# VectorE's small form of the wide expert job: limit raised to 160 tokens, work cut to 160 columns

## The reference, cut to what matters

```
def clamped_swiglu(hid):
    x_glu, x_lin = hid[..., ::2], hid[..., 1::2]
    x_glu = jnp.minimum(x_glu, SWIGLU_LIMIT)
    x_lin = jnp.clip(x_lin, -SWIGLU_LIMIT, SWIGLU_LIMIT)
    return x_glu * jax.nn.sigmoid(SWIGLU_ALPHA * x_glu) * (x_lin + 1.0)
...
        xb = h[toks]
        hid = xb @ w1[e] + b1[e]
        yb = clamped_swiglu(hid) @ w2[e] + b2[e]
        return yb * gts[:, None].astype(yb.dtype)
```

## Time and profile before

| what | value |
|---|---|
| median of 3 runs | 2038.56 us (2037.11 to 2043.55) |
| profiled execution, its own time | 2037.2 us |
| span of its trace | 2035.4 us |
| TensorE busy | 1977.3 us, 97% of the span |
| VectorE busy | 1385.7 us, 68% |
| experts' wide jobs, first to last product | 501.6 to 1307.9 us |
| experts' narrow jobs | 1307.9 to about 2020 us |

### The profile page before, as it was taken

The page is one execution under the profiler, slowest core; times in us unless marked ns, Lnnn a source line. Parts: engine busy times, 40 slices in busy tenths (PEclk is TensorE's granted clock), DMA queues, the critical chain, the costliest instruction groups (busy, mean ns, idle before and its releaser), DMA issues.

```text
span 2035.4 us, 29772 instructions
## 1 busy us (share of the span) xinstructions
PE 1977.3 (97%) x10588; PEld 1442.1 (71%) x10588; DVE 1385.7 (68%) x3952; ACT 385.3 (19%) x792; POOL 237.5 (12%) x313
## 2 busy tenths in 40 slices
PE   8999999997999999999999999999999999999996
PEld 5777777774999999999999999844444444444443
DVE  2666666663467777778877677687767776677765
ACT  1323233222012122222222222301101010001100
POOL 0221222221010011111111111100000000000000
PEclk9999999998999999999999999999999999999998
DMA  9311110004875687777888888999999999999992
GB/s 302 108 42 41 41 40 12 30 32 182 297 222 198 237 269 243 271 240 274 275 270 286 297 298 289 339 319 366 372 355 363 367 371 362 354 370 369 369 357 76
DMA packets 232241, 504.22 MB, mean 248 GB/s; under 512 B 7428, under 2 KB 14640, under 8 KB 230016
## 3 DMA queue, kind: packets, MB, share of 16 engines
q1 hardware_dynamic: 218496, 454.93, 62.6%
q0 software_dynamic: 11392, 40.18, 8.1%
q10 hardware_dynamic: 2304, 8.39, 1.0%
HBM read 475.48 MB, written 28.00 MB: 247 GB/s over the span
## 4 chain that ended last, share of the span: by engine, by line
issue 44%; PE 26%; DMA 2%; DVE 2%; POOL 1%; ACT 0%; POOLq 0%; DVEq 0%; ACTq 0%
PE ps_unit L1651 26%; DMA out_dram<-y_rows,idx_cur 2%; POOL x_got L1258 1%; DMA x_got<-h_rows,idx_next 0%; DVE act_T L1480 0%; DVE sig L1478 0%; DVE glu L1470 0%; ACT sig L1341 0%; PE ps_list L1623 0%; POOL carrier L1254 0%; POOL out_dram L1302 0%; POOL out_dram L1270 0%; POOLq L1194 0%; DVE match L1391 0%; DVE reached L1435 0%
## 5 line engine op out<-in xcount | busy, mean ns | idle before, releaser
L1651 PE MATMUL ps_unit<-xT,w_slot 128*128 128x136 f32 (+6 forms) x3840 | 526.6, 300 | 10.3 <-issue 8.7
L1651 PEld LDWEIGHTS ps_unit<-xT,w_slot 128*128 128x128 f32 x3840 | 521.3, 197 | 11.5 <-issue 11.4
L1675 PE MATMUL ps_unit<-w_slot,xT 128*128 128x512 f32 x1088 | 473.9, 593 | 0.0
L1675 PEld LDWEIGHTS ps_unit<-w_slot,xT 128*128 128x128 f32 x1088 | 205.3, 190 | 251.6 <-issue 251.6
L1183 DVE STREAM_TRANSPOSE xT<-x_got 32x256 f32<-32x256 f32 x668 | 291.0, 436 | 13.4 <-DMA x_got<-h_rows,idx_next 4.6
L1651 PE MATMUL ps_unit<-act_T,w_slot 128*128 128x136 f32 (+6 forms) x1920 | 264.1, 299 | 7.2 <-DVE act_T L1480 7.1
L1651 PEld LDWEIGHTS ps_unit<-act_T,w_slot 128*128 128x128 f32 x1920 | 259.4, 191 | 10.4 <-DVE act_T L1480 6.3
L1687 PE MATMUL ps_unit<-w_slot,act_T 128*128 128x512 f32 x544 | 239.3, 592 | 1.3 <-DVE act_T L1183 1.3
L1496 DVE STREAM_TRANSPOSE y_rows<-yT 32x256 f32<-32x256 f32 x396 | 172.6, 436 | 42.9 <-ACT yT L1348 37.6
L1183 DVE STREAM_TRANSPOSE act_T<-act_rows 32x64 f32<-32x64 f32 x816 | 192.6, 236 | 12.2
L1687 PEld LDWEIGHTS ps_unit<-w_slot,act_T 128*128 128x128 f32 x544 | 102.0, 190 | 123.6 <-issue 121.5
(11 more groups left out here) (262 smaller groups left out, 1604.3 us busy)
## 6 DMA issues: line engine op xcount, KB each, us to landing
w_slot<-in_w_dram SPq DMA_DIRECT2D x192, 2048.0 KB, 11.0
b_row<-in_b_dram SPq DMA_DIRECT2D x17, 1024.0 KB, 13.0
b_row<-in_b_dram SPq DMA_DIRECT2D x17, 512.0 KB, 15.3
w_in_sb<-in_w_in_dram SPq DMA_DIRECT2D x6, 1024.0 KB, 11.9
x_in<-in_x_dram SPq DMA_DIRECT2D x8, 512.0 KB, 3.4
x_res<-in_x_dram SPq DMA_DIRECT2D x8, 512.0 KB, 4.8
out_dram<-x ACTq DMA_DIRECT2D x8, 512.0 KB, 5.1
h_rows<-h ACTq DMA_DIRECT2D x8, 512.0 KB, 3.1
```

Source lines behind the costliest of these rows:

```text
L1651: last = pe.matmul(ps_unit[p % RING][:, u, 0:n], w, moving[:, k, 0:n], start=(k == 0), stop=(k == KD - 1))
L1675: last = pe.matmul(ps_hid[c], xT[:, k, 0:P], w_slot[:, c, k, :], start=(k == 0), stop=(k == KD - 1))
```

## The change

`small` goes from size 144 to size 160, so that VectorE's second loop also covers the two jobs of size 152 (there is none of size 160). The second block of small jobs moves 32 rows where it moved 16; for the two jobs of size 152 it is 32 rows where it was 64. `clip` and `finish` take a column count: 160 in the small form, 256 in the full one as before.

```diff
-    small = SIZES.index(144)
-    second_rows = ((small, 16), (SIZES.index(192), 64), (last_size, P))
+    small = SIZES.index(160)
+    second_rows = ((small, 32), (SIZES.index(192), 64), (last_size, P))
...
-            def clip(q, p):
+            def clip(q, p, n):
...
-                v.tensor_scalar(glu[:, p % 3, :], ps_unit[p % RING][:, 0, :], b1_cur[:, 2 * p:2 * p + 1], LIMIT,
+                v.tensor_scalar(glu[:, p % 3, 0:n], ps_unit[p % RING][:, 0, 0:n], b1_cur[:, 2 * p:2 * p + 1], LIMIT,
                                 ALU.add, ALU.min).then_inc(glu_ready[p].sem, 1)
...
-            def finish(q, p):
+            def finish(q, p, n):
...
-                v.tensor_tensor(sig[:, p % 3, :], sig[:, p % 3, :], glu[:, p % 3, :], ALU.mult).then_inc(scaled[p].sem, 1)
+                v.tensor_tensor(sig[:, p % 3, 0:n], sig[:, p % 3, 0:n], glu[:, p % 3, 0:n], ALU.mult).then_inc(scaled[p].sem, 1)
...
-                        finish(q, p - 1)
-                    clip(q, p)
+                        finish(q, p - 1, squares * Q)
+                    clip(q, p, squares * Q)
```

More of the change, by code:

```diff
@@ L1465, in _ @@
             match_tokens(0, bass.ds(first_expert, 1), base_row[:, 0:1])
-            def clip(q, p):
+            def clip(q, p, n):
                 wait(dve, unit_done[p], q)
-                v.tensor_scalar(glu[:, p % 3, :], ps_unit[p % RING][:, 0, :], b1_cur[:, 2 * p:2 * p + 1], LIMIT,
+                v.tensor_scalar(glu[:, p % 3, 0:n], ps_unit[p % RING][:, 0, 0:n], b1_cur[:, 2 * p:2 * p + 1], LIMIT,
                                 ALU.add, ALU.min).then_inc(glu_ready[p].sem, 1)
-                v.tensor_scalar(lin[:, p % 3, :], ps_unit[p % RING][:, 1, :], b1_cur[:, 2 * p + 1:2 * p + 2], LIMIT + 1.0,
+                v.tensor_scalar(lin[:, p % 3, 0:n], ps_unit[p % RING][:, 1, 0:n], b1_cur[:, 2 * p + 1:2 * p + 2], LIMIT + 1.0,
                                 ALU.add, ALU.min).then_inc(unit_read[p].sem, 1)
-            def finish(q, p):
+            def finish(q, p, n):
                 wait(dve, sig_ready[p], q)
-                v.tensor_tensor(sig[:, p % 3, :], sig[:, p % 3, :], glu[:, p % 3, :], ALU.mult).then_inc(scaled[p].sem, 1)
+                v.tensor_tensor(sig[:, p % 3, 0:n], sig[:, p % 3, 0:n], glu[:, p % 3, 0:n], ALU.mult).then_inc(scaled[p].sem, 1)
                 wait(dve, scaled[p], q)
-                v.scalar_tensor_tensor(out=act_T[:, p, :], in0=lin[:, p % 3, :], scalar=1.0 - LIMIT, in1=sig[:, p % 3, :],
+                v.scalar_tensor_tensor(out=act_T[:, p, 0:n], in0=lin[:, p % 3, 0:n], scalar=1.0 - LIMIT, in1=sig[:, p % 3, 0:n],
                                        op0=ALU.max, op1=ALU.mult).then_inc(act_ready[p].sem, 1)
@@ L1522, in wide_job @@
                         read_list(q + 1)
-                finish(q, P1 - 1)
+                finish(q, P1 - 1, squares * Q)
                 wait(dve, gathered_a, q + 1)
```

## The result

The changed kernel takes 2029.35 us (median of 5 runs, 2027.56 to 2029.93). The kernel before, in runs beside it, takes 2042.97 (5 runs, 2037.11 to 2043.55). The ratio is 0.9943 with a 95% interval of 0.9928 to 0.9959, which is 11.6 us (8.4 to 14.7); the two medians alone differ by 13.6. A second comparison on another chip gave 2028.58 against 2040.05 and 0.9946 (0.9933 to 0.9960). The forecast was 2031 and 6.7 us; the time lies in its range, the gain by the ratio was 1.7 times as large. By the two profiled executions, one of each kernel, the gain is 2037.2 - 2029.35 = 7.9 us.

The account below looks back on a forecast made before the run. TensorE, busy 97% of the span, was taken as the bound, with only its 7.1 us of waits for `act_T` to win. Gains of 4.74 + 1.93 = 6.67 us from 2037.2 gave 2030.5, put at 2031; range 2028 to 2036.

Parts of the forecast that it names:

- TensorE alone decides: TensorE is busy 97% of the span; a microsecond a wide job gives up there arrives at the end whole.
- part 1: Small form in both size-152 jobs: `turn_y` 5.40 us shorter, scatter earlier, waits behind them go; gain 4.74 us.
- 4.74 is all there is: Upper bound for the size-152 jobs' small form: TensorE's idle waits of 1.97 and 2.77 us behind them.
- If products became shorter: Closing remark: the forecast would err on the other side if TensorE's products shortened, which nothing in the trace suggested.
- Part 2: 160 columns in small jobs' clip and finish: operations 324 ns for 424, last piece's chain 0.30 us earlier; gain 1.93 us.
- Part 3: 32 rows for 16 in the second block of seven jobs: scatter lands 0.5 us later, hidden; no loss.
- the limit of 25.2 us: In a size-136 job, VectorE may resume up to 25.2 us in before TensorE has to wait.
- A: All waits of the nine small jobs for `act_T` gone: 2030 to 2032 us; chance 0.62.
- B: Columns save less, or the last piece's chain keeps its 0.2 to 0.3 us: 2032.2 to 2033.6 us; chance 0.17.
- C: Scatter lands late in some jobs, new waits of up to 3 us: 2033 to 2037 us; chance 0.13.
- E: Late scatter of size-152 jobs not due to `turn_y`; only 1.9 us from the columns: 2035 to 2037; chance 0.04.
- D: Slower: scattered rows all naming token 0 queue up, landings up to 22.5 us, about 2117 us; chance 0.02.

Follow-up runs that it names:

- experiment 1: Changed kernel (small form up to size 160, 32 rows), but clip and finish of every wide job on 256 columns; ratio to before 0.9973.
- experiment 7: Changed kernel with 128 rows in place of 32 in the second block of small jobs; ratio to before 0.9962.
- experiment 5: Changed kernel, but its small form turns 8 squares in `turn_x` in place of 5, `turn_y` staying at 5; ratio to before 1.0011.
- experiment 6: Changed kernel, but its small form turns 8 squares in `turn_y`, `turn_x` staying at 5; ratio to before 1.0059.
- experiment 4: The kernel before, unchanged, run again for a second profile; 2040.88 us, 3.7 above its first profiled execution.
- experiment 8: The changed kernel, unchanged, run again, giving its second profile; 2028.58 us against 2040.05 for the kernel before.
- experiment 2: Kernel before with only the 160 columns in clip and finish of small jobs; small form still ends at size 144 with 16 rows; ratio 0.9982.
- experiment 3: Kernel before with only 32 rows in place of 16 in the second block of jobs up to size 144; ratio 0.9994.

## Why the prediction was right, and where its sizes were off

- **TensorE alone decides, and a wide job's microsecond reaches the end whole.** Held: 9.4 us in the wide jobs less 1.5 in the mixer is the 7.8 of the spans, nearly to a tenth; the waits in the first narrow job stayed at 1.3 and 0.5 us.
- **The limit of `turn_y`, part 1.** The mechanism held: experiment 1 has the gain with the form and without the columns, experiment 7 with 128 rows, experiment 5 without the shorter `turn_x`, and experiment 6 loses part of it with the long `turn_y`. The size was wrong: the two jobs gained 2.51 and 4.64 us, of which 0.30 each belong to the columns, so 6.55 and not 4.74. The step that failed is "4.74 is all there is", and its mis-sized term is the 2.77 of the first job of size 144, which measured 4.34. I read the idle column of the earlier trace rows as the whole cost of VectorE being late. But the later products wait for piece 7, and the prediction had both numbers for it: 8.6 us from VectorE's resuming to the end of piece 7, so 1004.58 + 8.6 = 1013.2, where TensorE would have needed it at 1006.97 + 1.88 = 1008.85. That is 4.3 us. Products at half clock had filled the second wait, so no idle time showed it (experiment 4). The sign was in the row: 17.74 us for 128 records, where 1.88 and 14.23 make 16.1. "If products became shorter, which nothing in the trace suggests" passed over it. For the second job of size 152 the idle column gave 1.97 where 2.21 were won; that the rest lies in the modelled ends of products is my guess.
- **What I left out.** In other executions of the kernel before, the half clock costs time on top (2.35 us in the second profile). The nine small jobs took 437.95 and 441.81 us before and 428.43 and 428.13 after: 9.5 us gained in the first pair of profiles, 13.7 in the second.
- **The landing in part 1.** I moved the wait's end by 5.4 us and kept the landing. It moved by 9.5 (from 29.6 to 20.1 us into the first job of size 144), as the landing itself fell from 8.98 to 5.08 us. Fewer rows and an earlier start both stand behind that; experiment 6, with 32 rows and the late start, landed in 7.7 there, so by these single landings some 1.3 of the 3.9 us are the rows' and 2.6 the time's. It changed nothing, since the job had room.
- **Part 2, the columns.** `sig` and `act_T` took 324 and 325 ns, as forecast. The last piece's wait went in all six jobs behind a small one: 0.30 us each in place of 0.23 to 0.32. The two jobs of part 1 gained it too, and the first of size 152, where no wait stood in TensorE's rows: 0.30 x 9 and the 0.27 of the first job of size 136 make 2.97 for a forecast 1.93. With 6.55 that is 9.52, and 0.1 was lost in jobs of the full form.
- **Part 3, the rows.** Some 0.8 us on average for 16 rows where I took 0.5, within a spread of the landings of 2 us and more; hidden in all jobs of both profiles, up to the limit of 25.2 us, which experiments 6, 7 and 8 confirm. In the second profile one scatter landed in 10.06 us and VectorE resumed at 25.1, so hardly any room is left.
- **The median against the profile.** I set the forecast against the one profiled execution. The kernel before varies more than the changed one (2035 to 2047 us in 29 runs beside experiments 1 to 4), and that execution was among its fast ones. That the time came out within 2 us of 2031 is in part luck: beside the changed kernel, the one before had a median of 2042.97, some 5 us above where my sum began, and the gain was some 5 us larger than my sum, and the two errors cancel. The two profiles of each kernel give 808.3 and 795.8 us for the wide jobs, 12.5 apart, which fits the 11.6 of the runs.
- **The rivals.** A came true, with a larger sum. B, C and E fall: the waits are gone, the landings stayed below the limit, and the form carries the larger part (6.55 of 9.52 us). D falls by experiment 7. The forecast of 0.57 for faster was too shy, for a gain of which part lay outside the rows that I counted.

## What to carry to other kernels

The idle time ahead of one row need not be the whole cost of a late input: slow products can fill a second wait, or come on top of it. Compare the length of the rows behind the wait with that of equal rows elsewhere, and read the granted clock there. Set the time at which the last input was ready against the time at which it was needed. Weigh a job by the distance between its starts, which holds all of it. And where an off-path engine's tail decides (here transposes, gates, scatter), work out up to when it may end; that limit held better than any single gain.

## What the runs showed of the hardware that I had not expected

- Behind a wait of TensorE of 2.2 to 2.9 us for VectorE the granted clock was 0.50 for some 3 us, once for 7 (the first job of size 144 in both profiles of before and in experiments 2 and 3; experiment 5). It is no fixed price: the job lost at most 0.1 us by it in the first profile of before, some 0.6 us in experiment 2, 1.7 in experiment 5 and 2.35 in the second profile of before. Nor is it certain: a wait of 2.19 us in experiment 5 and one of 2.70 in the first profile of before had no such stretch behind them. Behind waits of 0.9 to 1.1 us in experiment 6 there was none.
- A loop that is jumped over costs TensorE 2.5 to 3.7 us at its own instructions, once 9.3, and at times a granted clock of 0.50 behind it. Without three such places the wide jobs took 7.8 to 10.1 us less, although a late VectorE came to light that costs 2.6 us in one of them.
- One and the same accumulating scatter lands in 5 to 10 us with 16 to 64 rows, by the moment in the job at which it is issued more than by its rows (about 0.025 us a row from 32 to 128).
- 120 rows of a scatter that all name one row of the output did not queue up: landings of 11.0 to 11.4 us with 128 rows, 8.4 to 9.0 with 32 (experiment 7).
